# The token factor of the first RMSNorm moved behind the projections, high products first, and a respaced head schedule, in one hybrid decoder layer

## The reference

```python
xn = rms_norm(h, norm1)                       # h * rsqrt(mean(h*h) + eps) * norm1
proj = xn @ w_in                              # q k v z (8 heads of 128), b a (8 each), sc_c sc_u sc_b, gate_a gate_b
q, k, v = silu(causal_conv4(q, k, v))
q, k = l2_normalize(q), l2_normalize(k)
o = chunk_gated_delta_rule(q, k, v, g(a), sigmoid(b))    # chunks of 64
y_a = (rms_norm(o, o_norm) * silu(z)) @ w_dn_out
y_b = (sc_b * causal_conv3(sc_c * sc_u)) @ w_sc_out
h = h + (sigmoid(gate_a) * y_a + sigmoid(gate_b) * y_b) @ w_o
gt, up = split(rms_norm(h, norm2) @ w_gate_up)
h = h + (silu(gt) * up) @ w_down              # width 2816
return rms_norm(h, final_norm)[16:]
```

## Time and profile before

| | |
|---|---|
| median of 3 runs | 1102.64 us (1101.8 to 1102.78) |
| the profiled execution | 1102.56 us, its span 1100.8 us |
| PE busy in the span | 1071.9 us, 97% |
| ACT, POOL, DVE busy | 456.7, 550.4, 345.7 us |
| granted PE clock, mean | 0.994 |

### The profile page before, as it was taken

How to read it: one execution, slowest core, us unless ns; L and a number is a source line. 1 busy time by engine, 2 the same in 40 slices (tenths; PEclk the granted TensorE clock), 3 DMA queues, 4 the chain that set the end, 5 groups by cost and what they waited for, 6 DMA issues and landing times.

```text
span 1100.8 us, 20365 instructions
## 1 busy us (share of the span) xinstructions
PE 1071.9 (97%) x8275; PEld 911.5 (83%) x8275; DVE 345.7 (31%) x642; ACT 456.7 (41%) x1063; POOL 550.4 (50%) x481
## 2 busy tenths in 40 slices
PE   7999999999999999999899999999999999999997
PEld 6989898889989898978788888878888888888886
DVE  6344545545454636361100112221212111100001
ACT  5655455554646463742422323443333322232232
POOL 4353544435353535363443655665555555555553
PEclk9999999999999999999999999999999999999998
DMA  4222212222212122112252232222232222232222
GB/s 180 75 82 66 81 59 68 78 69 63 84 60 87 59 70 76 59 59 78 77 172 96 88 104 81 93 95 96 96 96 96 96 96 94 91 103 94 86 89 77
DMA packets 28812, 95.45 MB, mean 87 GB/s; under 512 B 2984, under 2 KB 5288, under 8 KB 28720
## 3 DMA queue, kind: packets, MB, share of 16 engines
q1 hardware_dynamic: 27520, 91.77, 25.3%
q10 hardware_dynamic: 1200, 2.38, 0.7%
HBM read 92.03 MB, written 2.11 MB: 86 GB/s over the span
## 4 chain that ended last, share of the span: by engine, by line
PE 87%; DVE 6%; issue 4%; ACT 1%; POOL 1%; DMA 0%; DVEq 0%; POOLq 0%
PE bank L973 87%; DVE xd L696 1%; POOL w_lo L314 1%; DVE cv L876 1%; DVE um L776 1%; DVE am L696 1%; DVE raw L696 0%; DVE xd L747 0%; DVE qkv L701 0%; DVE qkv L709 0%; DVE cv L884 0%; ACT og_hi L403 0%; DVE cv L709 0%; DMA h_in<-h_t 0%; DVE tm L696 0%
## 5 line engine op out<-in xcount | busy, mean ns | idle before, releaser
L314 POOL TENSOR_TENSOR w_lo<-w_raw,w_hi 128x512 fp32r<-128x512 f32 x322 | 416.7, 1312 | 484.7 <-ACT w_hi L403 484.5
L973 PE MATMUL bank<-x_hi,w_hi 128*128 128x258 f32 (+2 forms) x896 | 248.9, 336 | 6.2 <-DVE x_lo L713 3.7
L973 PE MATMUL bank<-x_hi,w_lo 128*128 128x258 f32 (+2 forms) x896 | 230.8, 316 | 0.0
L973 PE MATMUL bank<-x_lo,w_hi 128*128 128x258 f32 (+2 forms) x896 | 230.7, 316 | 0.0
L403 ACT ACTIVATE w_hi<-w_raw 128x512 fp32r<-128x512 f32 x322 | 187.3, 620 | 97.5 <-PE bank L973 97.1
L973 PE MATMUL bank<-og_hi,w_hi 128*128 128x512 f32 x416 | 164.7, 396 | 0.0
L973 PE MATMUL bank<-og_lo,w_hi 128*128 128x512 f32 x416 | 164.3, 395 | 0.0
L973 PE MATMUL bank<-og_hi,w_lo 128*128 128x512 f32 x416 | 164.3, 395 | 0.0
L973 PEld LDWEIGHTS bank<-x_hi,w_hi 128*128 128x128 f32 x896 | 146.4, 189 | 20.7 <-issue 6.9
L973 PEld LDWEIGHTS bank<-x_hi,w_lo 128*128 128x128 f32 x896 | 147.6, 189 | 11.2
L973 PEld LDWEIGHTS bank<-x_lo,w_hi 128*128 128x128 f32 x896 | 147.9, 189 | 8.9
(11 more groups left out here) (260 smaller groups left out, 1285.8 us busy)
## 6 DMA issues: line engine op xcount, KB each, us to landing
w_raw<-w_stream SPq DMA_DIRECT2D x162, 512.0 KB, 3.3
h_in<-h_t SPq DMA_DIRECT2D x4, 528.0 KB, 5.0
h<-h_t ACTq DMA_DIRECT2D x1, 2048.0 KB, 10.0
h_in<-gc_dram SPq DMA_DIRECT2D x7, 264.0 KB, 3.1
out<-h SPq DMA_DIRECT2D x4, 256.0 KB, 3.2
out<-h SPq DMA_DIRECT2D x2, 384.0 KB, 2.8
cst<-consts SPq DMA_DIRECT2D x1, 512.0 KB, 8.1
h_in<-gc_dram ACTq DMA_DIRECT2D x1, 264.0 KB, 3.3
```

Source lines behind the costliest of these rows:

```text
L314: nc.gpsimd.tensor_tensor(low_weights(n)[:, at], w_raw[:, n % 3, at], high_weights(n)[:, at].bitcast(f32), ALU.subtract).then_inc(wlo_read ...
L973: return nc.tensor.matmul(o, w, x, start=start, stop=stop)
```

## The change

Eight things change.

1. Norm 1's token factor is not in the data any more. `x_hi` is the rounded product of h and norm1, made by ACT as soon as a part of h is there, and `x_lo` is made by DVE. The factor `rs1` gets memory of its own (`rs_mem`) and is applied by DVE where a projection leaves PSUM: q, k and v into `raw` (then a `tensor_scalar` on SBUF makes the scaled `cv`), z, c (twice, for c and u carry it both), gb and ga, and the token projections. The block sc takes the factor of b in a second multiplication.
2. The small vectors come first in SP's queue, the first weight block after the first part of h.
3. PE starts with `first_blocks`: the two products with high data of blocks 0 and 1, then the two blocks' products with low data, then the sums for `rs1`, then the token projections. Their turn is in block 2. The low weights of blocks 0 and 1 are DVE's, not POOL's.
4. ACT no longer evacuates q, k, v and c. Its Silu of z and its Sigmoid of the gates read SBUF, after DVE's multiplication. Gate buffers are `zs` and `egate` in turn.
5. The transpose `um` stands in step 0, ahead of the meta tokens' and the u block's work.
6. The output norm is respaced: root at step 2, DVE's two multiplications at step 7, `og_hi` at 8, `og_lo` at 9. After the last head the program asks for the Ln and Exp table ahead of the wait for the sums, and `TRAIL` is 10.
7. q by k moves from step 5 to step 10 and DVE's use of it to step 11. Its wait for `mu` is gone there, but the wait of the level at step 5 stays.
8. There are 16 warming matmuls in place of 28 and 9.

```diff
-            for k in range(KT):
+            def plain_high(k):
                 act.wait_ge(h_loaded[k // 2], 16)
+                nc.scalar.activation(x_hi[:, k, :], h_in[:, k, :], ACT.Copy,
+                                     scale=sm[:, NORM1 + k:NORM1 + k + 1]).then_inc(xhi_ready, 1)
+            act.wait_ge(small_in, 16)
+            plain_high(0)
+            plain_high(1)
             split_weights(0, 0)
             split_weights(0, 1)
+            for k in range(2, KT):
+                plain_high(k)
+            split_weights(1, 0)
+            split_weights(1, 1)
+            for k in range(KT):
+                square(k)
...
-                        if step == 1 and h >= 1:
+                        if step == 2 and h >= 1:
+                            if h == HEADS:
+                                nc.scalar.preload_act_table_set("natural_log_exp_and_others")
                             act.wait_ge(o_sums, h)
                             inverse_root(flat(osq), dbank[0][:, :], 1.0, 1).then_inc(o_root, 1)
-                        if step == 4 and h >= 1:
+                        if step == 8 and h >= 1:
                             act.wait_ge(ogf_ready, h)
...
                 if kind == "z":
-                    if m >= 2:
-                        act.wait_ge(oglo_ready, m - 1)
-                    nc.scalar.activation(zs[:, m % 2, :], p[0][:, :], ACT.Silu).then_inc(zs_ready, 1)
+                    act.wait_ge(z_scaled, m + 1)
+                    nc.scalar.activation(zs[:, m % 2, :], zs[:, m % 2, :], ACT.Silu).then_inc(zs_ready, 1)
...
+            first_low_weights(0)
+            for k in range(5):
+                plain_low(k)
+            first_low_weights(1)
+            for k in range(5, KT):
+                plain_low(k)
+            for k in range(1, KT):
+                add_square(k)
...
+                            dve.wait_ge(t_ready, h + 1)
+                            nc.vector.transpose(flat(um), flat(tm)).then_inc(u_ready, 1)
...
-                        if step == 1:
-                            dve.wait_ge(t_ready, h + 1)
-                            nc.vector.transpose(flat(um), flat(tm)).then_inc(u_ready, 1)
-                        if step == 5:
+                        if step == 11:
                             dve.wait_ge(qk_done, h + 1)
...
+                    for part, result in zip(token_halves(kind), p):
+                        ins = mult(raw[:, c % 2, 3 + part.start:3 + part.stop], result[:, 0:part.stop - part.start], rs1[:, part])
+                    ins.then_inc(raw_scaled, 1)
...
+                    nc.vector.tensor_scalar(cv[:, c % 2, first:], raw[:, c % 2, 3 + first:], sm[:, last:last + 1], None,
+                                            ALU.mult).then_inc(raw_ready, 1)
...
+                if kind == "z":
+                    if m >= 2:
+                        dve.wait_ge(ogf_ready, m - 1)
+                    mult(zs[:, m % 2, :], p[0][:, :], rs1[:, META:L]).then_inc(z_scaled, 1)
+                if kind == "c":
+                    if m:
+                        dve.wait_ge(yblo_ready, m)
+                    for part, result in zip(token_halves(kind), p):
+                        ins = mult(cbuf[:, part], result[:, 0:part.stop - part.start], rs1[:, part])
+                    link(ins)
+                    mult(cbuf[:, TAIL:L], cbuf[:, TAIL:L], rs1[:, TAIL:L]).then_inc(c_ready, 1)
...
+                    mult(gates[i % 2], p[0][:, :], rs1[:, META:L]).then_inc(gate_scaled, 1)
...
+            def first_blocks():
...
+                for n in range(2):
+                    parts, to = outs(n)
+                    for k in range(KT):
+                        if k % 4 == 0:
+                            wait_low(pe, n, k // 4)
+                        pe.wait_ge(xhi_ready, k + 1)
+                        for w in (w_hi, w_lo):
+                            for o, s in zip(to, parts):
+                                mm(o, w[:, n, k * 128:(k + 1) * 128], x_hi[:, k, s], start=k == 0 and w is w_hi, stop=False)
+                for n in range(2):
+                    parts, to = outs(n)
+                    for k in range(KT):
+                        pe.wait_ge(xlo_ready, k + 1)
+                        for o, s in zip(to, parts):
+                            ins = mm(o, w_hi[:, n, k * 128:(k + 1) * 128], x_lo[:, k, s], start=False, stop=k == KT - 1)
+                    ins.then_inc(block_done, 1)
+                pe.wait_ge(x_added, KT - 1)
+                for s in range(2):
+                    ins = mm(dbank[2 + s][:, 0:HALF], ones, sums1[:, s * HALF:(s + 1) * HALF])
+                ins.then_inc(x_sums, 1)
...
-                        if step == 5:
-                            pe.wait_ge(qkv_ready, 3 * h + 1)
-                            pe.wait_ge(mu_ready, h + 1)
...
-                            if l == 1 and h:
+                            if l == MASKED and h:
                                 pe.wait_ge(ogf_ready, h)
```

More of the change, by code:

```diff
@@ L269, in _ @@
         def _(sp):
+            sp.dma_start(sm[:, :], small[:, :]).then_inc(small_in, 16)
             for part in range(4):
                 sp.dma_start(h_in[:, 2 * part:2 * part + 2, :], h_t[:, 2 * part:2 * part + 2, :]).then_inc(h_loaded[part], 16)
-            sp.dma_start(sm[:, :], small[:, :]).then_inc(small_in, 16)
-            for n in range(STREAM):
+                if part == 0:
+                    sp.dma_start(w_raw[:, 0, :], w_stream[0, :, :]).then_inc(w_in[0], 16)
+            for n in range(1, STREAM):
                 if n == 2:
@@ L315, in split_weights @@
                                         ALU.subtract).then_inc(wlo_ready, 1)
-            split_weights(0, 0)
-            split_weights(0, 1)
-            for k in range(1, KT, 2):
-                pool.wait_ge(xhi_ready, k + 1)
-                nc.gpsimd.tensor_tensor(x_lo[:, k, :], xnf[k % 4], x_hi[:, k, :].bitcast(f32),
-                                        ALU.subtract).then_inc(xlo_ready, 1)
             def level_mask(l):
@@ L328, in delta_steps @@
                     for step in range(0 if h >= 0 else PRE, STEPS if h < HEADS else TRAIL):
-                        if step == 5 and h >= 1:
+                        if step == 9 and h >= 1:
                             pool.wait_ge(oghi_ready, h)
@@ L426, in _ @@
             for s in range(2):
-                nc.scalar.activation(rs1[:, halves[s]], big[0][s][:, 0:HALF], ACT.Ln, scale=1.0 / D,
+                nc.scalar.activation(rs1[:, halves[s]], dbank[2 + s][:, 0:HALF], ACT.Ln, scale=1.0 / D,
                                      bias=eps[:, 0:1]).then_inc(act_chain, 1)
@@ L606, in evacuate @@
+                    nc.scalar.activation(gates[i % 2], gates[i % 2], ACT.Sigmoid).then_inc(ge_ready, 1)
                 if kind == "gate" and m == 0:
@@ L696, in mult, with plain_low, first_low_weights, add_square @@
                 return nc.vector.tensor_tensor(to, a, b, ALU.mult)
-            for k in range(1, KT):
+            def plain_low(k):
+                dve.wait_ge(xhi_ready, k + 1)
+                nc.vector.scalar_tensor_tensor(x_lo[:, k, :], h_in[:, k, :], sm[:, NORM1 + k:NORM1 + k + 1],
+                                               x_hi[:, k, :].bitcast(f32), ALU.mult, ALU.subtract).then_inc(xlo_ready, 1)
+            def first_low_weights(n):
+                for half in range(2):
+                    at = slice(512 * half, 512 * half + 512)
+                    dve.wait_ge(whi_ready, 2 * n + half + 1)
+                    nc.vector.tensor_tensor(w_lo[:, n % 2, at], w_raw[:, n % 3, at], w_hi[:, n % 2, at].bitcast(f32),
+                                            ALU.subtract).then_inc(wlo_first, 1)
+            def add_square(k):
                 dve.wait_ge(x_squared, k + 1)
@@ L744, in delta_steps @@
                     for step in range(0 if h >= 0 else PRE, STEPS if h < HEADS else TRAIL):
-                        if step == 3 and h >= 1:
+                        if step == 7 and h >= 1:
                             dve.wait_ge(o_root, h)
@@ L983, in _, with outs @@
                 mm(dbank[3][:, 0:128], ones, ones)
-            pe.wait_ge(x_added, KT - 1)
-            for s in range(2):
-                ins = mm(big[0][s][:, 0:HALF], ones, sums1[:, s * HALF:(s + 1) * HALF])
-            ins.then_inc(x_sums, 1)
-            for _ in range(WARM // 3):
-                mm(dbank[3][:, 0:128], ones, ones)
+            def first_blocks():
+                def outs(n):
+                    parts = token_halves(BLOCKS[n][0])
+                    return parts, [big[n][s][:, 0:part.stop - part.start] for s, part in enumerate(parts)]
+                for n in range(2):
[15 more added lines that the diff above has]
+                pe.wait_ge(x_added, KT - 1)
+                for s in range(2):
+                    ins = mm(dbank[2 + s][:, 0:HALF], ones, sums1[:, s * HALF:(s + 1) * HALF])
+                ins.then_inc(x_sums, 1)
             def token_projections():
```

(10 more changed lines are left out.)

164 lines of the change are left out of this document (71 added, 93 removed).

## The result

The changed kernel takes 1094.42 us (median of 4 runs, 1094.10 to 1096.09), beside 1102.71 us of the kernel before on the same chip: a ratio of 0.9929, 95% interval 0.9912 to 0.9946. It is faster by 8.3 us, where the forecast was 10.85 (1091.8). The page of its profiled execution (span 1092.4 us, granted clock 0.998) has

What follows compares the result with a forecast made beforehand. PE, busy 97%, was taken as the bound, so only its waits count. Terms -11.0, -1.9, -4.0, -4.9, +10.0 and +0.95 give -10.85, from 1102.64 to 1091.8 us; range 1077 to 1099.

Steps and rivals of the forecast that it cites:

- B: Hand-over from b to q block: PE's wait for um goes, but raw, freeing q's bank, then binds; -1.9 us.
- E: c block, seven heads: z's multiplication behind kd_vb on DVE delays vnew and the u block's low weights; +10.0 us.
- A: Start: reordered transfers and products let block 2 begin at 26.3, with DVE's sums last; -11.0 us.
- C: PE's wait for mu in seven heads goes, as og_hi and q by k move to later steps; -4.0 us.
- D: Last head's norm: PE's wait and the half clock behind it go with table, root and weights reordered; -4.9 us.
- F: First gate: DVE's multiplication, table load and Sigmoid delay copies mpb and h_in, so PE waits; +0.95 us.
- Costed at nothing: Effects priced at zero: ACT's lost copies, and DVE's added 4.5 us a head, 36 us in all, said to fit.
- About 1.7: Sign of being right: in seven heads PE waits about 1.7 us for POOL's w_lo in front of u.
- the first (E hidden, 1081.8): Rival: z's multiplication runs early, so the c block's delay does not show; 1081.8 us, chance 0.2.
- The second (DVE the bound): Rival: k and v taps or updates on DVE queue behind POOL's halves, 2.6 us a head; 1112.6 us, chance 0.1.
- The third rival: The start gains less, through half clock for one or two stretches and late sums; 1095 us, chance 0.1.

Runs made afterwards that it cites:

- experiment 3: Changed kernel with the transpose um back in step 1, behind the meta tokens' operations; 1093.92 us.
- experiment 4: Changed kernel with the transpose um one place later on DVE in step 0, behind ma and ahead of mkdec and mvb; 1089.81 us.
- experiment 7: Changed kernel without the Ln and Exp table asked for ahead of the last head's sums, root still at step 2; 1094.62 us.
- experiment 1: Changed kernel with DVE's multiplication of z ahead of the delta's step 20 (kd_vb) instead of behind it; 1085.38 us.
- experiment 2: Changed kernel with z's Silu straight from PSUM on ACT and no multiplication of z by the token factor; 1083.66 us.
- experiment 12: Changed kernel with z's and gates' multiplications ahead of the delta's step, um behind ma, mkdec and mvb in step 1, weights first in c blocks; 1073.73 us.
- experiment 9: Changed kernel with 2 instead of 16 warming steps; 1095.48 us.
- experiment 8: Changed kernel with the last head's root back at step 1 and no table asked for ahead of it; 1099.85 us.
- experiment 10: Changed kernel with the first weight block again behind all four parts of h in SP's queue; 1098.25 us.

## Why the prediction was right, and where it was off

The direction, the range and the mechanisms of five parts held; the gain is 2.5 us smaller than forecast, and nearly all of that is part B. E came out 0.9 cheaper than forecast and head 0 cost 0.7 that was not in the sum, which nearly cancel, by luck.

- **A** (forecast -11.0, measured -10.7). Block 2 starts at 26.36 for 26.3; the first product at 8.13 is 0.4 later than I had it, and PE's low products end 0.6 later (21.25 for 20.6), which DVE's sums at 21.46 just cover. The turn costs 1.6 in its new place (27.08 to 28.67) for 1.3: that is the 0.3.
- **B** (forecast -1.9, measured +0.5). This is the step that failed: "it is raw that frees the bank for the q block", taken for the only thing that could be late next. I followed what um had been behind on DVE, and not what came to stand behind um. ma did, 0.7 later, and through malev on POOL the first half of q's low weights, later than raw by 0.4 (181.31 and 180.93). The row was there to be read: in the kernel before, these weights ended 0.1 before um (experiment 3). Experiments 3 and 4 show it from both sides.
- **C** (-4.0, -3.9) and **D** (-4.9, -5.0) held in size and cause; in D I gave the table a part, and experiment 7 gives it none.
- **E** (forecast +10.0, measured +9.1 in seven heads). Each link came where it was put: vnew's copy runs right behind the table load, PE waits 0.35 for it and then 1.27 for the low weights. "About 1.7" stands among the signs for the second wait, but the sum itself has 1.43 - 0.3 + 0.3 = 1.43 there. The forecast counted seven heads. Head 0 has no recurrence beside its c block, but the same chain z, silu, table load, squares, weights, and pays 0.7. Experiments 1 and 2 show that in the seven heads the place is the whole price.
- **F** (0.95, 0.83). The gate's multiplication, the table load and the Sigmoid stand ahead of mpb, as forecast.
- **Costed at nothing.** DVE's 77 us more are over twice the 36 that I had counted, and made PE wait nowhere but in the places above. The 4.5 us a head were right for q, k, v and z (35.8 us in all), but the "four for c" were named and not added: they are 19.7 us. The gates' multiplications are another 11, those of sc 7, and the taps of q, k and v are 11.5 us longer. The start, which DVE also had before, is 5 us shorter.

Of the rivals, the first (E hidden, 1081.8) was false by order, and became true when the order was changed: experiment 1. The second (DVE the bound) has its mechanism in the trace but not its price. The taps of 528 columns went from 0.90 to 0.98, those of 512 from 0.76 to 1.08, and c's second multiplication runs in 1.78 us beside POOL's w_lo and in 0.83 when that has nearly ended. In the timelines, first the changed kernel (POOL busy from 223.09 to 225.60), then experiment 1 (POOL busy to 221.43):

```profile
224.37 1.78 DVE L681 TENSOR_TENSOR cbuf<-cbuf,rs_mem 128x516 f32<-128x516 f32 x1
```

```profile
221.16 0.83 DVE L681 TENSOR_TENSOR cbuf<-cbuf,rs_mem 128x516 f32<-128x516 f32 x1
```

The two end 0.55 us after POOL's instruction does (226.15 and 225.60, 221.98 and 221.43), and so does this multiplication in all eight heads of both kernels, to 0.01, whether it starts 0.05 or 1.0 us behind the start of POOL's instruction. With POOL idle, in seven heads of experiment 12, all of it takes 0.70. So these rows look like a DVE instruction that stands still until the POOL instruction that was there first has ended, not like one that runs at a lower speed. That agrees with what the "GPSIMD Engine Reference" of the Trainium skill says in section 8 (Key points), that GpSimd and VectorE contend where the latter has two SBUF inputs; PE waits for neither. The third rival's number (1095) is nearer to the measured 1094.4 than the forecast's, but not by its mechanism: the start gained what was forecast, the half clock did not happen there, and experiment 9 shows that it would have cost nothing.

The drain that the page "ScalarE: Activation LUTs" of the Trainium skill (section What ACT_TABLE_LOAD costs) adds to each load is not seen here either: the load at 219.23 is followed by vnew 1.29 us later, and E came out at 1.3 a head and not at the 2.8 that the page's figure would give as an estimate.

## What to carry to other kernels

When an instruction is moved forward in an engine's order, list what now stands behind it and follow each to the engine that waits last, across other engines too; the wait that shows in a trace can hide a second one that ends 0.1 or 0.4 us sooner. Work moved to an idle engine is free or dear by the place it gets in that engine's order, so look for the operation it was put behind before it is judged by its length. When a wait is priced, take off the hand-over that stays without it (0.23 around a group of small matmuls here), and add up every instruction that the change adds before an engine is called free.

## What was not expected of the hardware

The granted clock fell to 0.50 for 3.41 us at PE's wait of 3.38 us (experiment 8, from 530.95, 0.27 before PE goes on) and after an idle time of 4.14 us (experiment 10, from 13.36, 1.0 after PE had gone on at 12.33). The kernel before has both forms: from 535.31, 1.2 after PE went on at 534.15, and from 16.49, within an idle time of 2.50 us that ends at 16.99. Behind the wait of 1.9 us near 47 us it stayed at 1.0 in the profiled executions of the changed kernel and of the eight experiments beside it that have this wait, and fell in that of experiment 9, at 1.6 us more. One of the four runs of the changed kernel is 1.7 us longer (1096.09) with a mean clock of 0.996 and not 0.997 to 0.998; that would fit the same fall, but its trace was not taken.
